# The last expert block merged by TensorE with place matrices, and y loads that wait for the scatter before it

## What is computed

```python
    for e in range(N_EXPERTS):
        hid = jax.nn.silu(t @ w_gate[e]) * (t @ w_up[e])
        out = out + combine[:, e:e + 1] * (hid @ w_down[e])
...
    x = x + _hier_moe(_rmsnorm(x, g_ffn), w_coarse, b_coarse, w_fine, b_fine, w_gate, w_up, w_down)
y_prompt = _rmsnorm(xp, g_final)
y_sample = _rmsnorm(xs, g_final)
```

## Time and profile before

| what | us |
|---|---|
| three runs | 536.95, 540.36, 541.76 |
| median | 540.36 |
| span of the profiled execution | 539.0 |
| PE busy | 483.3 (90% of the span) |
| DVE busy | 237.7 (44%) |
| POOL busy | 183.3 (34%) |
| ACT busy | 100.4 (19%) |

### The profile page before, as it was taken

How to read it: one execution, slowest core, us unless ns; L and a number is a source line. 1 busy time by engine, 2 the same in 40 slices (tenths; PEclk the granted TensorE clock), 3 DMA queues, 4 the chain that set the end, 5 groups by cost and what they waited for, 6 DMA issues and landing times.

```text
span 539.0 us, 8928 instructions
## 1 busy us (share of the span) xinstructions
PE 483.3 (90%) x3301; PEld 285.3 (53%) x3302; DVE 237.7 (44%) x514; ACT 100.4 (19%) x204; POOL 183.3 (34%) x282
## 2 busy tenths in 40 slices
PE   6999999999999999999679998989898982998884
PEld 3787777777777545545334443444443441443331
DVE  4219999999964422245821222222122210221246
ACT  5131011002104423324301111101111110011223
POOL 3010817647394600111234443333443332234101
PEclk9989999999999999999789999999999996999999
DMA  8995006100000597023959799999999999999477
GB/s 328 310 391 142 0 2 258 54 2 0 1 1 1 189 412 315 39 69 124 403 192 420 284 411 422 402 397 421 419 418 419 417 419 420 420 418 421 195 272 256
DMA packets 35509, 141.25 MB, mean 262 GB/s; under 512 B 10080, under 2 KB 10096, under 8 KB 23193
## 3 DMA queue, kind: packets, MB, share of 16 engines
q1 hardware_dynamic: 29194, 127.91, 60.4%
q0 software_dynamic: 4960, 9.45, 4.7%
q10 hardware_dynamic: 1327, 3.49, 1.8%
HBM read 134.47 MB, written 13.17 MB: 274 GB/s over the span
## 4 chain that ended last, share of the span: by engine, by line
PE 71%; DMA 12%; DVE 5%; issue 5%; SPq 3%; ACT 2%; POOL 1%; DVEq 0%; POOLq 0%; ACTq 0%
PE bank L1284 26%; PE bank L1367 10%; PE bank L1485 9%; PE bank L1505 8%; PE bank L1480 8%; DMA region_x<-in_w_up 5%; DMA region_w<-in_w_in 3%; PE bank L1277 2%; DMA slot<-y_rows 2%; SPq L402 2%; PE bank L1495 2%; PE bank L1433 1%; DVE ua L1169 1%; PE bank L1393 1%; DVE ua L1171 1%
## 5 line engine op out<-in xcount | busy, mean ns | idle before, releaser
L1284 PE MATMUL bank<-region_h,region_w 128*128 128x256 f32 (+1 forms) x576 | 142.3, 409 | 0.0
L1284 PEld LDWEIGHTS bank<-region_h,region_w 128*128 128x128 f32 x576 | 110.2, 192 | 30.5 <-issue 0.8
L1169 DVE TENSOR_TENSOR ua<-ua,bank 128x128 f32<-128x128 f32 x30 | 8.7, 288 | 174.2 <-ACT ua L639 174.2
L1367 PE MATMUL bank<-region_w,z 128*128 128x512 f32 x128 | 56.7, 596 | 0.2 <-ACT z L584 0.2
L1505 PE MATMUL bank<-region_w,ua 128*32 128x512 f32 x328 | 50.3, 598 | 3.3 <-DVE ua L1171 3.3
L928 DVE SCALAR_TENSOR_TENSOR z<-ub,par,z 128x512 f32<-128x512 f32 x60 | 48.7, 812 | 0.0
L928 DVE SCALAR_TENSOR_TENSOR region_x<-ub,par,region_x 128x512 f32<-128x512 f32 x56 | 45.9, 820 | 0.0
L1485 PE MATMUL bank<-region_w,z 128*32 128x256 f32 x512 | 45.1, 403 | 0.2 <-issue 0.2
L792 POOL COPY gcol<-gidx 128x1 uint32 (+1 forms) x30 | 5.4, 180 | 108.9 <-DVE sb_rows L1158 108.9
L723 POOL TENSOR_TENSOR ub<-region_x 128x512 f32<-128x512 f32 x4 | 20.2, 5056 | 63.8 <-ACT ub L538 32.6
L1485 PE MATMUL bank<-slot,z 128*32 128x256 f32 x192 | 25.9, 425 | 14.5 <-DMA region_w<-in_w_up 9.9
(11 more groups left out here) (244 smaller groups left out, 647.5 us busy)
## 6 DMA issues: line engine op xcount, KB each, us to landing
region_w<-in_w_down SPq DMA_DIRECT2D x21, 1024.0 KB
region_w<-in_w_gate SPq DMA_DIRECT2D x16, 1024.0 KB
region_w<-in_w_up SPq DMA_DIRECT2D x16, 1024.0 KB, 15.7
region_w<-in_w_in SPq DMA_DIRECT2D x4, 2048.0 KB, 19.5
slot<-in_w_gate SPq DMA_DIRECT2D x6, 1024.0 KB, 14.8
slot<-in_w_up SPq DMA_DIRECT2D x6, 1024.0 KB
slot<-in_w_down SPq DMA_DIRECT2D x6, 1024.0 KB
region_x<-in_w_up SPq DMA_DIRECT2D x5, 1024.0 KB
```

What stands on the lines that cost most here:

```text
L1284: ins = mm(ps[2 * bank + j][:, 0:LEN[j]], sec[name][:, k, c * P:(c + 1) * P], hT[:, k, CUT[j]], start=(k == 0), stop=(k == KC - 1))
L1367: ins = mm(ps[2 * (t % 2) + j][0:n, :], z[:, k, t * P:t * P + n], w_out_sb[:, k, j * 512:(j + 1) * 512], start=(k == order[0]), stop=(k == ...
```

## The change

The last block is no longer scattered and loaded back. ACT copies its result to `ylast` in SBUF. For each tile PE multiplies it by a place matrix `sel`, which holds at (place in the block, token) the token's weight, and so adds the last block's part in PSUM. The block has two halves of 64 partitions (columns 0 to 511 of the result in the first, 512 to 1023 in the second), so each tile takes two matmuls with 64 rows of contraction, into two banks. The matrices are built by DVE behind the weights `w12` (ten scalings and five additions of 128x128), transposed by PE and copied back by ACT. Rows of `y_rows` that the last block would have written are zeroed early by a scatter of zeros (`nothing`, `s_clear`). SP waits only for the scatters of the blocks before the last. The y rows now go to slots 3 and 2 and not to slots 0 and 3. Tile 2 is finished in PSUM as well (`IN_PSUM`), tiles 0 and 4 get the last block's part by DVE additions from PSUM (`merge`). The x1 matmuls of tiles 1 and 3 move ahead of the loop of rounds, the fillers at the end go from 32 to 8, and ACT makes the bias of the root.

```diff
-FINISH = (0, 2, 1, 4, 3)
+FINISH = (0, 1, 2, 4, 3)
+IN_PSUM, BY_DVE = (1, 2, 3), (0, 4)
+FINAL = {0: (1, 2), 1: (4, 5), 2: (3, 0), 3: (6, 7), 4: (1, 2)}
...
-        yg = [[(SLOT0 if k == 0 else RW)[:, t * D:(t + 1) * D] for t in range(NT)] for k in range(2)]
+        yg = [[RW[:, lo + t * D:lo + (t + 1) * D] for t in range(NT)] for lo in (0, 2 * SEC + 3 * PART)]
...
-            sp.wait_ge(s_ysc[1], pairs * 16)
-            sp.wait_ge(s_ysc[0], (pairs + odd) * 16)
-            for t, k in ((0, 0), (0, 1), (2, 0), (1, 0), (2, 1), (1, 1), (4, 0), (4, 1), (3, 0), (3, 1)):
+            sp.wait_ge(s_clear, 16)
+            sp.wait_ge(s_ysc[1], pairs1 * 16)
+            sp.wait_ge(s_ysc[0], (pairs1 + odd1) * 16)
+            for t, k in ((0, 0), (0, 1), (2, 0), (2, 1), (1, 0), (1, 1), (4, 0), (4, 1), (3, 0), (3, 1)):
...
+            act.wait_ge(s_selT, 1)
+            nc.scalar.activation(sel[:, 0:4 * P], ps[6][:, :], ACT.Copy)
+            nc.scalar.activation(sel[:, 4 * P:NTOK], ps[7][:, 0:NTOK - 4 * P], ACT.Copy).then_inc(s_sel, 1)
...
+            gated(total)
+            act.wait_ge(s_hout, 16 * 5)
+            act.wait_ge(s_down, total)
+            nc.scalar.activation(ylast, ps[3][:, :], ACT.Copy).then_inc(s_ylast, 1)
...
+            pool.memset(nothing, 0.0).then_inc(s_nothing, 1)
             pool.wait_ge(s_ab, 1)
             pool.memset(RX[:, 0:D], 0.0).then_inc(s_stage, 1)
...
+            pool.indirect_dma_start(y_half, bass.IndirectOffsetOnAxis(ap=slast[:, 0:1], axis=0), nothing, None,
+                                    bounds_check=4 * NTOK - 1, oob_is_err=False).then_inc(s_clear, 16)
-            for b in range(2):
-                scatter_last(b, b, pairs * 2 + b)
-            with pool.If(odd > 0):
-                scatter_last(2, 0, pairs * 2 + 2)
+            with pool.If(odd1 > 0):
+                scatter(pairs1 * 2, 0, pairs1 * 2 + 2)
...
+            for t in range(NT):
+                if t >= 2:
+                    dve.wait_ge(s_selin, t - 1)
+                for k, dst in enumerate((onehot[t % 2], sel_in[:, t, :])):
+                    ins = nc.vector.tensor_scalar(dst, rplace, rplf[:, 2 * t + k:2 * t + k + 1], wlast[:, 2 * t + k:2 * t + k + 1],
+                                                  ALU.is_equal, ALU.mult)
+                link(ins)
+                nc.vector.tensor_tensor(sel_in[:, t, :], sel_in[:, t, :], onehot[t % 2], ALU.add).then_inc(s_selin, 1)
...
+            def merge(t):
+                n = TROWS[t]
+                dve.wait_ge(s_fin, summed[t])
+                dve.wait_ge(s_lastin, BY_DVE.index(t) + 1)
+                for j in range(2):
+                    xh = x1[0:n, t, j * 512:(j + 1) * 512]
+                    nc.vector.tensor_tensor(xh, xh, ps[FINAL[t][j]][0:n, :], ALU.add).then_inc(s_merge, 1)
...
+            def last_block(t):
+                n = TROWS[t]
+                for h in range(2):
+                    ins = mm(ps[FINAL[t][h]][0:n, :], sel[h * T:(h + 1) * T, t * P:t * P + n], ylast[h * T:(h + 1) * T, :],
+                             start=t in BY_DVE, stop=True)
+                return ins
```

More of the change, by code:

```diff
@@ L136, in build_step @@
         xrow = sb_rows[:, 0:D // 2]
+        ylast = sb_rows[:, D // 2:D]
         st_p = pst
@@ L816, in _ @@
             pool.memset(scol[:, :], 0).then_inc(s_si, 1)
[L818 to L820 removed]
+            pool.tensor_copy(slast[:, 0:1], sidx[:, bass.ds(total - 1, 1)]).then_inc(s_sl, 1)
             for g in range(2, 4):
@@ L1540, in _ @@
             tokens(0, KC // 2).then_inc(s_xt_ps, 1)
+            for t in range(NT):
+                n = TROWS[t]
+                pe.wait_ge(s_selin, t + 1)
+                ins = tr(ps[6 + t // 4][:, (t % 4) * P:(t % 4) * P + n], sel_in[0:n, t, :], ident[0:n, 0:n])
+            ins.then_inc(s_selT, 1)
             end = 0
@@ L1545, in _, with residual @@
                 end = last
+            def residual(t):
+                n = TROWS[t]
+                for j in range(2):
+                    mm(ps[FINAL[t][j]][0:n, :], ident[0:n, 0:n], x1[0:n, t, j * 512:(j + 1) * 512], start=True, stop=False)
+            pe.wait_ge(s_sel, 1)
+            pe.wait_ge(s_diag, 2 * len(BY_PE))
+            for t in BY_PE:
+                residual(t)
             with pe.Fori(1, NE // NSLOT) as it:
```

132 lines of the change are left out of this document (77 added, 55 removed).

## The result

The kernel after takes 544.09 us (median of 9 runs, 541.03 to 545.20), the kernel before 539.79 us beside it (9 runs, 536.95 to 541.76). The ratio is 1.0083, with an interval of 1.0060 to 1.0105. The profiled execution spans 542.7 us against 539.0. The forecast of the median was 539.9. So the change costs 4.3 us where 0.5 us of gain was forecast. The time lies inside the outer range of 534.5 to 545, but outside the forecast's own of 537.5 to 542, and on the other side of the kernel before.

What follows compares the result with a forecast made beforehand. The last block's scatter, the y loads behind it, tile 3's matmuls and final scaling bound the end; weights set the loop's end. 539.0 + 2.6 + 0.4 + 0.1 - 3.6 = 538.5 span; median 539.9, range 534.5 to 545.

Steps and rivals of the forecast that it cites:

- C: Stretch from the last block's first down matmul to the kernel's end; forecast to change by -3.6 us.
- The y rows' pace: Tail: 1.6 us for each full y load, giving 516.1 for the fifth and 517.7 for the sixth.
- The pair of merge matmuls: PE's tail: two matmuls of 64 contraction rows overlap and take 0.95 us; 1.8 kept as the alternative.
- Rival 1: PE's tail: the merge halves do not overlap, 3.4 us more on PE's new end, 543.3; chance 0.22.
- PE's last merge to the end: Final stretch: squares, root and scaling, 6.4 us before, plus 0.3 for ACT making the bias: 6.7 us.
- The x1 matmuls ahead of the loop: Before the loop: moved matmuls make PE 2.6 us late and every load behind the dry place at 346 moves 2.6.
- Rival 2: Expert loop: the moved x1 matmuls cost nothing, since the weight stream or PE's spare time absorbs them; 537.3, chance 0.13.
- POOL's memset: Routing part: a 128x512 memset of 0.5 us delays three DVE instructions; 0.4 us added.
- The place matrices: Routing part: DVE builds them in 4.2 us, inside its idle time before the gather lands; 0.1 us added.
- rival 4: Routing part: DVE and POOL block each other while the place matrices are built; 548.8, chance 0.10.
- A: Routing stretch, from DVE's 490-column operation to the first copy of gathered rows; forecast to change by +0.5 us.
- B: Stretch from the first copy of gathered rows to the last block's first down matmul; forecast to change by +2.6 us.

## Why the prediction was wrong, point by point

*The end was forecast at -3.6 us and came at +1.15.* This is the step that failed, 4.75 us of it, and it has two halves. With the clock kept up C is 29.74 us, against the forecast's 26.9. The sizes below are from one profile of each kernel; C itself differs by 1.6 us between two profiles of one and the same kernel (28.38 and 29.99), and with the three profiles of this end in which the clock fell (31.12, 31.67, 32.54) the clock's part comes to 1.4 to 2.8.

- The clock, 1.9 us, was not in the sum at all. The working had the wait in it ("wait for the y rows of tile 1 until 516.1", 2.2 us; it was 2.96) and priced it as time only. The kernel before covers just this place with 32 fillers, 7.07 us of them; the change leaves 8. To see that the fillers had been cut to a quarter and to ask what they were for was the missed reading. The x1 matmuls that left this place were cover as well: in the kernel before, without them, the clock fell even with all 32 fillers.
- The y rows' pace, 1.9 us. "1.6 us for each full one" was taken from before's waits, and gave 9.4 us for the fifth row and 11.0 for the sixth. They came at 10.4 and 12.9. Part of the reason is tile 4: its loads of 64 partitions run at half the rate and slow what stands beside them, and with them last the sixth row came at 11.3. It isn't the whole reason. In the kernel before tile 4's loads stand in the same place, at 205 to 262 GB/s from 524 to 527, and the sixth row still came at 11.1 (525.32 less 514.24). What else slowed it in the changed kernels stays open.
- The rest: 0.4 from the first y load, later by that much against the last block, and 0.6 from terms on PE's new end that were each a little short (a pair of merge matmuls 1.06 instead of 0.95, x1 of tile 2 at 1.9, a full tile 3.6 to 3.7).

*The pair of merge matmuls.* Right: the two row halves overlap. Eight instructions of L1622 take 2.13 us, 1.06 us for a pair; without overlap it would be 1.8. Rival 1 falls. The Trainium skill, "TensorEngine Tiling (Array Packing)", section Tiling Modes, says that tiles of the array operate independently of each other. The trace agrees, though a pair costs 1.06 us and not quite the 0.88 of one full matmul.

*PE's last merge to the end, 6.7 us.* Right: 536.0 to 542.7.

*The x1 matmuls ahead of the loop, 2.6 us.* Right in size and in mechanism: PE was 2.7 us late at the loop's start, the weight queue's hole was 2 us longer, and 2.1 us remained at the loop's end. Rival 2 falls. Only "every load behind it moves 2.6 us" was a little too strong.

*POOL's memset, 0.4 us.* Right: the three DVE operations beside it took 2.16 us instead of 1.70, and 1.70 again with the memset moved away.

*The place matrices, 0.1 us.* The chain itself was sized well, 4.95 us against 4.2 forecast, and DVE and POOL did not block each other (POOL's two fetches beside it took 1.29 and 1.01 us, before 1.30 and 1.01), so rival 4 falls. The cost was 1.46 us all the same. "DVE was idle from there to 273.58" counted 4.87 us of wait as free. It was not: the two register loads, 1.34 us, lay in it. They are not counted as busy and so have no time in a row, though the order of DVE's code has them (L1150, L1151); the chain pushed them out into the open. A rose by 1.99 us where 0.5 was forecast, 1.46 of it here.

*Rival 3, the release carries through,* did not happen in any kernel: the best C is 28.35 us, 2.2 below before, with the loads released 6.9 us sooner against the last block. PE then waits for rows or for DVE. Its sum has a slip: with rival 2 only the 2.6 us come back and not 3.1, so it should end at 533.7, not 533.2.

The sum, with what was measured: A +1.99, B +1.87, C +1.15, less 1.31 ahead of them. Against the forecast that is 1.49 too much in A, 0.73 too little in B, 4.75 too much in C and 1.31 less ahead of them: 4.2 us, the 542.7 of the profile less the forecast's 538.5.

That the time still lies inside the outer range, 0.8 us from rival 1's 543.3, is luck: rival 1's mechanism, merge halves that don't overlap, did not happen.

## What to carry to other kernels

When a change removes or shortens work that kept an engine busy ahead of a wait, price what the engine's clock does in that wait, not the wait alone; count the fillers of both versions, and the work that left the place. When one stretch of two profiles is compared, look first whether its matmuls had the same clock. Idle time in a row is not room for new work until the register loads and other things that are not counted as busy have been taken out of it. And when loads are released sooner, the order and the width of the loads decide what the release is worth: ask which row each engine takes first, and what a half-width load does to its neighbours.

## What the runs showed of the hardware that I had not expected

- The granted clock fell to 1.2 GHz 2.1, 2.4, 3.0 and 5.1 us behind PE's last matmul in four kernels, and stayed there for 6.8 us in the first three and 3.4 in the fourth. Eight matmul instructions took 6.65, 6.04 and 6.24 us instead of 3.6 to 3.7 in the first three.
- The same kernel part can meet either clock: the first block's gate matmuls ran in part at 1.2 GHz in the kernel before and at full speed in the kernel before with x1 early, 1.3 us apart, which hid most of a cost of 2.1 us.
- Two matmuls with 64 rows of contraction on the two halves of the array, 512 columns of f32 into two banks, take 1.06 us together.
- Loads of 64 partitions ran at 184 GB/s with the DMA engines at a share of 1.06, against 418 GB/s for full ones, and slow the loads beside them: the sixth row came at 12.9 us with them in the middle and at 11.3 with them last.
- A gather of rows landed 3.4 to 5.2 us behind its issue in five executions, whose kernels differ ahead of it in the place of one memset at most.
